# A down-projection by seven block products: four of eight feature pairs instead of three

## The reference, cut to what matters

```python
f = jnp.square(jax.nn.relu(u @ w_up[l])) @ w_down[l]     # (256, 8192) @ (8192, 2048)
h = h + rms_norm(f, g_post_mlp[l])
```

## Time and profile before

| | |
|---|---|
| median of 3 runs | 2031.14 us (2030.65 to 2031.42) |
| the profiled execution | 2031.48 us, of which the span is 2029.7 us |
| PE busy | 2017.8 us, 99% of the span, 10509 matmuls |
| DVE busy | 1489.5 us, 73% |
| ACT busy | 985.2 us, 49% |
| mean granted clock of TensorE | 0.999 |
| HBM read | 385.02 MB, 191 GB/s over the span |

### The profile page before, as it was taken

The page is one execution under the profiler, slowest core; times in us unless marked ns, Lnnn a source line. Parts: engine busy times, 40 slices in busy tenths (PEclk is TensorE's granted clock), DMA queues, the critical chain, the costliest instruction groups (busy, mean ns, idle before and its releaser), DMA issues.

```text
span 2029.7 us, 28875 instructions
## 1 busy us (share of the span) xinstructions
PE 2017.8 (99%) x10509; PEld 1719.2 (85%) x10509; DVE 1489.5 (73%) x2016; ACT 985.2 (49%) x1275; POOL 83.0 (4%) x91
## 2 busy tenths in 40 slices
PE   9999999999999999999999999999999999999998
PEld 7888898888888888999888888888888888888886
DVE  6766766566756655578999856587877887788887
ACT  6645444565544544433444644554553453354343
POOL 0000102001002000002000000000000000000001
PEclk9999999999999999999999999999999999999999
DMA  9688655655667665555666566655576466467554
GB/s 346 198 202 185 177 157 174 187 175 173 185 198 245 185 196 179 175 177 160 189 198 199 177 219 185 192 166 174 185 236 188 158 206 217 155 207 227 187 198 134
DMA packets 265475, 389.32 MB, mean 192 GB/s; under 512 B 12504, under 2 KB 147032, under 8 KB 264571
## 3 DMA queue, kind: packets, MB, share of 16 engines
q1 hardware_dynamic: 262587, 377.19, 60.9%
q0 software_dynamic: 2624, 10.54, 1.9%
q10 hardware_dynamic: 144, 0.01, 0.0%
HBM read 385.02 MB, written 2.54 MB: 191 GB/s over the span
## 4 chain that ended last, share of the span: by engine, by line
PE 98%; SPq 1%; DMA 1%; DVE 0%; ACT 0%; issue 0%; DVEq 0%
PE acc L701 18%; PE acc L678 17%; PE acc L680 17%; PE acc L679 17%; PE acc L699 10%; PE acc L692 2%; PE acc L691 2%; PE acc L693 2%; PE acc L697 1%; PE aux L730 1%; PE aux L732 1%; PE aux L731 1%; PE acc L730 1%; PE acc L731 1%; PE acc L732 1%; PE aux L1619 1%
## 5 line engine op out<-in xcount | busy, mean ns | idle before, releaser
L532 DVE TENSOR_TENSOR low_rows<-stage_rows,high_rows 128x1024 fp32r<-128x1024 f32 x480 | 575.2, 1210 | 295.6 <-ACT high_rows L518 286.9
L518 ACT ACTIVATE high_rows<-stage_rows 128x1024 fp32r<-128x1024 f32 x480 | 495.5, 1040 | 542.2 <-PE acc L680 480.8
L518 ACT ACTIVATE w_high<-stage 128x1024 fp32r<-128x1024 f32 (+1 forms) x264 | 276.1, 1047 | 405.1 <-PE acc L701 298.0
L532 DVE TENSOR_TENSOR w_low<-stage,w_high 128x1024 fp32r<-128x1024 f32 (+1 forms) x264 | 319.8, 1221 | 176.1 <-ACT w_high L518 171.5
L701 PE MATMUL acc<-u,w_high 128*128 128x512 f32 x900 | 247.9, 394 | 0.0
L701 PE MATMUL acc<-hT,w_high 128*128 128x512 f32 x645 | 177.5, 394 | 0.0
L701 PEld LDWEIGHTS acc<-u,w_high 128*128 128x128 f32 x900 | 152.9, 189 | 19.0
L699 PEld LDWEIGHTS acc<-u,w_low 128*128 128x128 f32 x960 | 146.8, 188 | 20.5
L699 PE MATMUL acc<-u,w_low 128*128 128x256 f32 x960 | 152.5, 281 | 0.0
L678 PE MATMUL acc<-high_rows,hT 128*128 128x512 f32 x384 | 151.8, 395 | 0.0
L680 PE MATMUL acc<-high_rows,hT 128*128 128x512 f32 x384 | 149.6, 390 | 0.0
(11 more groups left out here) (451 smaller groups left out, 3601.4 us busy)
## 6 DMA issues: line engine op xcount, KB each, us to landing
stage_rows<-in_w_in SPq DMA_DIRECT2D x160, 512.0 KB, 3.8
stage<-in_w_in SPq DMA_DIRECT2D x136, 512.0 KB, 3.6
stage_rows<-in_w_down SPq DMA_DIRECT2D x128, 512.0 KB, 4.4
stage<-in_w_up SPq DMA_DIRECT2D x120, 512.0 KB, 4.5
stage_rows<-in_w_o SPq DMA_DIRECT2D x64, 512.0 KB, 4.1
stage_rows<-in_w_pool_out SPq DMA_DIRECT2D x16, 512.0 KB, 3.9
stage_rows<-in_w_conv_out SPq DMA_DIRECT2D x16, 512.0 KB, 4.4
stage_rows<-in_w_mem_kv SPq DMA_DIRECT2D x14, 512.0 KB, 11.2
```

The lines of the kernel that those rows point to most:

```text
L518: act.activation(high[:, pr, k_from:kt, 0:p.cols], src[:, slot, k_from:kt, 0:p.cols], ACT.Copy).then_inc(high_done, 1)
L532: dve.tensor_tensor(low[:, pr, k_from:kt, 0:p.cols], src[:, slot, k_from:kt, 0:p.cols], high[:, pr, k_from:kt, 0:p.cols].bitcast(F32), ALU ...
```

## The change

Pairs 2, 3, 5 and 6 are done by seven products instead of 2, 4 and 6. A step of w_down has 24 slabs then, where it had 22, and the order of its pairs is: plain 0 and 1, seven 2, seven 3, plain 4, seven 5, seven 6, plain 7.

The kept rows are not added up by VectorE any more. Ahead of a step, ScalarE writes the rows kept in `z_rows` into the banks `aux` (`lay_z`: four copies, in the second step of a quarter at slabs 0 and 1, for the first step in the stage w_up before, at slabs 4 and 5); TensorE goes on summing in the banks (no start flag, from step 2 on; it waits for `z_laid` at the first LEFT); and after each step ScalarE copies the banks out (`keep_z`, in all quarters). Of the place of `f_sums` in memory one part is moved, since it is larger by a third.

```diff
--- before.py
+++ after.py
@@ -128,7 +128,7 @@
 
 
 LEFT, RIGHT, OUTER, INNER = "left", "right", "outer", "inner"
-SEVENS = (2, 4, 6)
+SEVENS = (2, 3, 5, 6)
 SEVEN_ORDER = ((0, 1), (2,), (3,), (4,), (5,), (6,), (7,))
 
 
@@ -278,7 +278,8 @@
         u2 = at("u2", Z + 48, [P, KT, 2, T], F32R)
         f_pair = at("f_pair", Z + 84, [P, KT, 2, T], F32R)
         y_rows = at("y_rows", Z + 16, [P, 2, D])
-        f_sums = at("f_sums", Z + 32, [P, len(SEVENS), 2, 4, P], F32R)
+        sums_at = [(Z + 32 + 4 * e, Z + 34 + 4 * e) for e in range(3)] + [(74.25, 82.75)]
+        f_sums = [[at(f"f_sums{e}{half}", kb, [P, 4, P], F32R) for half, kb in enumerate(places)] for e, places in enumerate(sums_at)]
         f_raw = at("f_raw", 72.25, [P, 4, P])
         z_at = ((Z + 44, Z + 46, Z + 80, Z + 82), (Z + 116, Z + 118, Z + 120, 80.75))
         z_rows = [[at(f"z_rows{step}{b}", kb, [P, ROW]) for b, kb in enumerate(places)] for step, places in enumerate(z_at)]
@@ -712,24 +713,24 @@
             (_, one, _), (_, two, _) = (job.group(i, u, part) for part in range(2))
             if kind == LEFT:
                 pe.wait_ge(s("f_sums_ready"), len(SEVENS) * int(job.name[-1]) + e + 1)
-                if e == 0 and step:
-                    if step <= 2:
-                        pe.wait_ge(s("z_copied"), 4 * step)
-                    else:
-                        pe.wait_ge(s("z_summed"), 4 * (step - 2))
+                if e == 0 and step == 1:
+                    pe.wait_ge(s("z_copied"), 4)
+                elif e == 0 and step:
+                    pe.wait_ge(s("z_laid"), 4 * (step - 1))
             pe.wait_ge(split_done, STAGES + n + 1)
             x1, x2 = ([p.rows[:, k0, half, 0:P] for half in range(2)], [p.rows[:, k0 + 1, half, 0:P] for half in range(2)])
             x4 = [p.rows[:, k0 + 1, half, P:2 * P] for half in range(2)]
-            sums = [[f_sums[:, e, half, r, :] for half in range(2)] for r in range(4)]
+            sums = [[f_sums[e][half][:, r, :] for half in range(2)] for r in range(4)]
             products = {LEFT: [(0, x1, aux[:, 0, :], True), (1, x2, acc[:, 2 * one, :], False)],
                         RIGHT: [(1, sums[3], acc[:, 2 * two, :], False)],
                         OUTER: [(turned, sums[1], aux[:, 1, :], True), (1 - turned, sums[0], aux[:, 3, :], True)],
                         INNER: [(0, sums[2], aux[:, 2, :], True), (1, x4, acc[:, 2 * one + 1, :], False)]}[kind]
             for k, (x_high, x_low), bk, own in products:
                 high, low = high_rows[:, pr, k, :], low_rows[:, pr, k, :]
-                pe.matmul(bk, x_high, high, start=own and e == 0, stop=False)
-                pe.matmul(bk, x_high, low, start=False, stop=False)
-                mm = pe.matmul(bk, x_low, high, start=False, stop=own and e == len(SEVENS) - 1)
+                laid = own and step >= 2
+                pe.matmul(bk, x_high, high, start=own and e == 0 and not laid, stop=False, skip_group_check=laid)
+                pe.matmul(bk, x_high, low, start=False, stop=False, skip_group_check=laid)
+                mm = pe.matmul(bk, x_low, high, start=False, stop=own and e == len(SEVENS) - 1, skip_group_check=laid)
             mm.then_inc(used, 1)
 
         def group_done(eng, job, i, u, part=0):
@@ -1437,7 +1438,7 @@
             def beside_last(n):
                 r = SQUARE_ROWS_AT.get(n)
                 if r is not None:
-                    act.wait_ge(s("z_summed"), 21)
+                    act.wait_ge(s("z_spread"), 1)
                     down_squares(r)
 
             def down_squares(r):
@@ -1452,20 +1453,35 @@
                         act.wait_ge(s("chain_var"), 11 + t)
                         act.activation(out_rs[:, t:t + 1], out_rs[:, t:t + 1], ACT.Sqrt).then_inc(s("chain_root"), 1)
 
-            def copy_z(q):
+            def lay_z(q, step, banks):
+
+                act.wait_ge(s("z_copied"), 4 * (2 * q + step))
+                for b in banks:
+                    act.activation(aux[:, b, :], z_rows[step][b][:], ACT.Copy).then_inc(s("z_laid"), 1)
+
+            def keep_z(q):
                 job = jobs[f"w_down{q}"]
                 inner = max(idx for idx, kind in enumerate(job.kinds) if kind == INNER)
 
                 def beside(n):
                     step, idx = n // job.S, n % job.S
-                    for b in {inner: (0, 1), inner + 2: (2, 3)}.get(idx, ()):
+                    if q and step and idx < 2:
+                        lay_z(q, step, (2 * idx, 2 * idx + 1))
+                    for b in {inner: (0, 1), inner + 1: (2, 3)}.get(idx, ()):
                         act.wait_ge(used, PAIRS + job.slab0 + step * job.S + inner + 1)
                         act.activation(z_rows[step][b][:], aux[:, b, :], ACT.Copy).then_inc(s("z_copied"), 1)
                 return beside
 
+            def lay_first(q):
+
+                def beside(n):
+                    if n in (4, 5):
+                        lay_z(q, 0, (2 * n - 8, 2 * n - 7))
+                return beside
+
             for q in range(4):
-                rounding(f"w_up{q}", beside=beside_up0 if q == 0 else None)
-                rounding(f"w_down{q}", beside=copy_z(q) if q == 0 else None)
+                rounding(f"w_up{q}", beside=lay_first(q) if q else beside_up0)
+                rounding(f"w_down{q}", beside=keep_z(q))
             rounding("w_down_last", last_down, beside=beside_last)
 
 
@@ -2576,8 +2592,8 @@
                 link(dve.tensor_tensor(f_raw[:, 0:2, :], f[:, 0:4:3, :], f[:, 1:2, :].to_broadcast([P, 2, P]), ALU.subtract))
                 link(dve.tensor_tensor(f_raw[:, 2, :], f_raw[:, 1, :], f[:, 0, :], ALU.add))
                 link(dve.tensor_tensor(f_raw[:, 3, :], f[:, 2, :], f_raw[:, 2, :], ALU.subtract))
-                link(dve.tensor_copy(f_sums[:, e, 0], f_raw[:]))
-                dve.tensor_tensor(f_sums[:, e, 1], f_raw[:], f_sums[:, e, 0].bitcast(F32), ALU.subtract).then_inc(s("f_sums_ready"), 1)
+                link(dve.tensor_copy(f_sums[e][0][:], f_raw[:]))
+                dve.tensor_tensor(f_sums[e][1][:], f_raw[:], f_sums[e][0][:].bitcast(F32), ALU.subtract).then_inc(s("f_sums_ready"), 1)
 
             def down_body(q, name, first=0):
                 job = jobs[name]
@@ -2615,32 +2631,15 @@
                     link(dve.tensor_tensor(y21, y21, z7[:], ALU.add))
                     link(dve.tensor_tensor(y22, y22, z5[:], ALU.subtract))
 
-            def sum_z(q):
-                job = jobs[f"w_down{q}"]
-                inner = max(idx for idx, kind in enumerate(job.kinds) if kind == INNER)
-
-                def beside(n):
-                    step, idx = n // job.S, n % job.S
-                    for b in {inner + 1: (0, 1), inner + 2: (2, 3)}.get(idx, ()):
-                        if b == 0:
-                            dve.wait_ge(used, PAIRS + job.slab0 + step * job.S + inner + 1)
-                            if q == 1:
-                                dve.wait_ge(s("z_copied"), 4 * (step + 1))
-                            else:
-                                dve.wait_ge(s("z_summed"), 8 * (q - 2) + 4 * (step + 1))
-                        v = z_rows[step][b]
-                        dve.tensor_tensor(v[:], aux[:, b, :], v[:], ALU.add).then_inc(s("z_summed"), 1)
-                return beside
-
             def spread(name, step, n):
                 if n in SPREAD_AT[name]:
-                    dve.wait_ge(s("z_summed"), 16 if step else 20)
+                    dve.wait_ge(s("z_copied"), 24 if step else 28)
                     z_spread(step, SPREAD_AT[name].index(n))
 
             def beside_last(n):
                 spread("w_down_last", 0, n)
                 if n == SPREAD_AT["w_down_last"][-1]:
-                    dve.sem_inc(s("z_summed"), 1)
+                    dve.sem_inc(s("z_spread"), 1)
 
             def last_down():
 
@@ -2673,7 +2672,7 @@
             splitting("w_up_first", first_body, beside=beside_first, at_once=True)
             for q in range(4):
                 splitting(f"w_up{q}", up_body(f"w_up{q}", 0 if q else 2), 3, beside=sums_up(q), at_once=True)
-                splitting(f"w_down{q}", down_body(q, f"w_down{q}"), beside=sum_z(q) if q else None, at_once=True)
+                splitting(f"w_down{q}", down_body(q, f"w_down{q}"), at_once=True)
                 if q == 0:
                     dve.wait_ge(s("h2_squared"), 8)
                     link(dve.tensor_reduce(eps_3, sums_3, AX, ALU.add))
```

## The result

The changed kernel takes 2049.79 us (median of 6 runs, 2048.55 to 2051.19), the one before 2030.89 us beside it (2030.51 to 2031.71). The ratio is 1.0093, with a 95% interval of 1.008 to 1.0106: slower by 18.9 us. The forecast was 2048.2 us.

The account below looks back on a forecast made before the run. TensorE, busy 88.00 of 88 us in the down-projections, was taken to bound the kernel. New waits of 21.8 us less 4.76 us saved gave +17.1 on 2031.14: 2048.2 us, range 2042 to 2056.

Parts of the forecast that it names:

- The gain: 21 matmuls by 0.2267, 4.76 us: TensorE in w_down: one more pair takes 7 products instead of 8 in each of 7 steps, saving 4.76 us.
- The wait at OUTER of every second seven, 1.41 us, and its restart, 0.15 us: TensorE at a couple's second OUTER: ready at 8.21, wanted at 6.80; 1.56 us with restart, 14 times, 21.8 us.
- The start at 2.71: VectorE starts the second seven's LEFT 2.71 us after the first's first matmul, set by a buffer; a 5.50 us chain follows.
- rival A: The cover holds at the second seven's OUTER, so only the gain is left: 2026.4 us; chance 0.08.
- The pitch of 1.14 us against a full duration of 1.22: Queued VectorE operations start 1.14 us apart; counting 1.22 would add 0.16 us per couple, 2 us in all.
- INNER just in time: 0: Second seven's INNER: low part ready at 9.44, TensorE wants it at 9.50; counted 0, up to 0.3 us in the range.
- C: Larger waits: INNER's margin fails (4.2 us) and ScalarE's copies cost 5 us: 2057.4 us; chance 0.07.
- Writes and copies by ScalarE: 0: ScalarE's 20 writes into banks and 28 copies out, near 0.585 us each, are hidden: 0; 5 us if cover failed.
- The feature sums in w_up: 0: One more pair's feature sums cost VectorE 2.3 us per w_up stage; counted 0, at worst 1.0 us once in w_up3.
- DMA: 0: Loads and bytes per step stay; the tightest load in a step lands at 12.6, wanted near 18: 0.
- B: Smaller waits: half of each wait at OUTER is absorbed, +6.2 us, 2037.3 us; chance 0.07.
- D: TensorE's clock falls to 1.2 GHz for 12 matmuls after each of 14 waits, +38 us: 2086 us; chance 0.03.

Follow-up runs that it names:

- e7_sums_ahead_two_couples: Changed kernel with the addition for OUTER and the first for INNER moved earlier on VectorE, pair order kept: 2027.76 us, ratio 0.9983 to the kernel before.
- e3_outer_ahead: Changed kernel with only the addition for OUTER moved on VectorE, ahead of the low part of the slab before LEFT: 2033.61 us, ratio 1.0012 to the kernel before.
- e2_scalar_alone: Changed kernel with sevens 2, 4, 6 only, keeping ScalarE's writes and copies of kept rows: 2030.91 us, ratio 1.0 to the kernel before.
- e1_one_couple: Changed kernel with sevens 2, 3, 5, so three sevens and one back-to-back couple a step: 2042.35 us, ratio 1.0056 to the kernel before.
- e6_order: Changed kernel with four sevens (2, 3, 4, 6) reordered so only 3 and 4 stand back to back: 2039.34 us, ratio 1.0042 to the kernel before.
- e5_order_and_sums_ahead: Changed kernel with sevens 2, 3, 4, 6, only 3 and 4 adjacent, and OUTER's and the first INNER addition moved earlier: 2027.62 us, ratio 0.9985 to the kernel before.
- e8_loads_not_held: Changed kernel with SyncE issuing each next w_up load once its own buffer is free: 2050.81 us, ratio 1.0094 to the kernel before.
- e4_sums_on_gpsimd: Changed kernel with all additions of weight blocks for OUTER and INNER given to GpSimd: 2066.63 us, ratio 1.0175 to the kernel before.

## Why the prediction was right, point by point

**The gain: 21 matmuls by 0.2267, 4.76 us.** Right in count (10488 against 10509). The two runs without waits in w_down show -3.4 and -3.3 us in the time, not -4.8, and the rows say where the rest is. From the first LEFT to the start of the last matmul TensorE takes 591.89 us in the kernel before and 588.27 in e7_sums_ahead_two_couples, 3.62 us less. The other 1.14 us lie nearly all at the second seven of each couple: 10.25 us from its LEFT to the next instead of 10.20 in the couple 2, 3, and some 0.1 us too long in the couple 5, 6, where the second matmul of OUTER starts up to 0.30 us after the first. Its low part is ready only some 0.1 us ahead; why that costs a restart isn't shown. So the price of 0.2267 us a matmul holds, and what fits so narrowly isn't quite free.

**The wait at OUTER of every second seven, 1.41 us, and its restart, 0.15 us.** Right in place, number and size. The wait seen is 1615.74 less 1614.27, 1.47 us, with another 0.11 at the second matmul and some 0.02 in the matmuls after: 1.60 against 1.56. The rows say 14 x 1.60 = 22.4 us, I had 21.8. The first experiment shows the position to be the cause, the third shows that the chain is: what is taken out of it comes off the wait at full length.

The start at 2.71 was the step that the whole forecast hung on (the buffer, not VectorE's time). It is at 2.72. Had it been a question of VectorE's time, moving the sum would have returned nothing. That the buffer sets this start is read from the rows: ScalarE begins 1.62 after t = 0 in both kernels, each time released by the products' last line. No run gave it a fifth buffer, which would test it directly. "Idle time before it can't be used", which the prediction held against rival A, is true of the order in this code only: e3_outer_ahead used that very time.

**The pitch of 1.14 us against a full duration of 1.22.** The rows after have 1611.33 and 1612.47 for the outer sum, again 1.14, and the wait came out as summed by it. The Trainium skill, "VectorE: DVE Perf Modes", section "The DRAIN you can't avoid", says first that an operation doesn't start before the pipe of the former is empty. Taken as the full duration at the two places that the prediction names, that gives an estimate of 8.37 for the end of the chain; it is at 8.23. (The 14 couples would make 2.2 us of it, where the prediction says 2.) The same section goes on that an operation which isn't held starts earlier, which the prediction left out; the rows agree, and by how much had to be read from them.

**INNER just in time: 0.** Right: no wait before INNER in any of the 14. But the sum had a slip. With OUTER begun at 8.28 its six matmuls of 1.36 us end at 9.64, not 9.50. In the rows INNER's low part is ready at 9.43, as forecast (9.44), and INNER begins at 9.76: the margin is 0.33 us instead of 0.06, so that C's first half was less near than it seemed.

**Writes and copies by ScalarE: 0.** Right, shown by e2_scalar_alone. The write into a bank, which no trace of before had, took 0.583 us, and I had taken 0.585.

**The feature sums in w_up: 0.** No wait stands there.

**DMA: 0.** This term was wrong, by 0.9 us. I looked for the tightest load within a step. The one that mattered is at the step's end: SyncE's program holds the first loads of the next w_up until the inner sums of the last seven are through. In the trace after, at the edge of w_down2 and w_up3, the last inner sum is on VectorE at 1852.19, for 0.69 us, and SyncE's row of loads begins 0.41 behind its end; the loads land some 4 us later, and ScalarE waits for them. SyncE, VectorE's sum, ScalarE:

```profile
1853.29 7.37 SPq L506 DMA_DIRECT2D stage<-in_w_up  x8
```

```profile
1852.19 0.69 DVE L551 TENSOR_TENSOR stage_rows<-stage_rows 128x512 f32<-128x512 f32 x1
```

```profile
1857.19 1.06 ACT L519 ACTIVATE w_high<-stage 128x1024 fp32r<-128x1024 f32 x1 [1.32 <-DMA stage<-in_w_up]
1858.99 1.06 ACT L519 ACTIVATE w_high<-stage 128x1024 fp32r<-128x1024 f32 x1 [0.73 <-DMA stage<-in_w_up]
```

And what came of it, on VectorE (the additions to y_rows) and on TensorE:

```profile
1861.23 1.28 DVE L2612 TENSOR_TENSOR y_rows<-acc,y_rows 128x512 f32<-128x512 f32 x2
```

```profile
1862.14 0.39 PE L681 MATMUL acc<-high_rows,f_pair 128*128 128x512 f32 x1
1862.70 0.49 PE L698 MATMUL acc<-u,w_high 128*128 128x512 f32 x1 [0.17 <-DVEq L2614]
```

ScalarE had to wait 1.32 and 0.73 us for weights of w_up, where the kernel before has no wait for a DMA at this edge (at that of w_down0 and w_up1 it has two, of 0.30 and 0.69 us, and no gap of TensorE). So VectorE's low parts, which stand ahead of the additions to y_rows on its queue, were late, the additions ended at 1862.5, and TensorE's first product of w_up, which needs their bank, started at 1862.70 instead of 1862.37, with 0.1 us of restart. At the three edges that makes 0.35, 0.1 and 0.43 us. In e1_one_couple, e6_order and e5_order_and_sums_ahead, whose steps do not end in a couple, there is no such gap, and in e8_loads_not_held, which takes the hold away and leaves all else, it is gone at all three edges. What stays open is why the time of that run did not show it.

The account: 14 x 1.60 + 0.9 - 4.76 = 18.5 us; the start of the kernel was 0.4 us quicker in this execution; 18.1 us is the difference of the spans. The median's 18.9 us lies within the spread of the runs about that.

**The rivals.** A (the cover holds) did not occur here, and its point of decision was the right one: the chain had to fit into the 4.09 us between 2.71 and 6.80. In e7_sums_ahead_two_couples 3.56 us of it are left behind LEFT, with 3.69 to be had from its start at 3.11, and it fits. B and C were sizes, and the forecast's own was met. D, the clock, stayed at 0.999 in spite of 14 waits of 1.3 us.

## What to carry to other kernels

Where engines hand slabs through a ring of buffers, an average (VectorE busy in 76 of 88 us) says nothing of a burst: take the item whose buffer frees last, add the chain behind it in the order of the queue, and compare with the time until it is wanted. A cheaper product that needs more preparation costs time where two of them stand back to back, and the cure is to find the piece of preparation that needs no buffer and to put it into the idle time ahead. Two additions moved ahead did it here: 22.0 us, with no work saved.

## What the runs showed of the hardware

GpSimd's additions slow VectorE's subtractions when both work on this memory. With the additions running beside it in e4_sums_on_gpsimd, VectorE's subtraction of 1024 columns took 1.746 us on average instead of 1.222, and work worth 73 us on VectorE cost 94 us there when it was given away. The Trainium skill, "GPSIMD Engine Reference", section "Specifications", names the shared access and contention with VectorE instructions of two SBUF inputs, as these are; this trace agrees, and the factor of 1.4 to 2.1 on the average is its own.

The average hides how it comes about. Two subtractions that follow each other on VectorE, and GpSimd's addition, which begins between their starts:

```profile
1622.17 1.22 DVE L531 TENSOR_TENSOR low_rows<-stage_rows,high_rows 128x1024 fp32r<-128x1024 f32 x1
1623.31 3.43 DVE L531 TENSOR_TENSOR low_rows<-stage_rows,high_rows 128x1024 fp32r<-128x1024 f32 x1
```

```profile
1622.82 2.84 POOL L544 TENSOR_TENSOR stage_rows<-stage_rows 128x1024 f32<-128x1024 f32 x1 [8.51 <-DMA stage_rows<-in_w_down]
```

The addition ends at 1625.66 and the second subtraction at 1626.74, 1.08 later. So it is with every subtraction in w_down that took longer than in the changed kernel: 50 of 1024 columns end 1.08 or 1.09 us after the end of an addition, 18 of 512 columns 0.55 us after it, whenever they began; the others took 1.26 us at most, and 0.68. They look as if they had stood still until the addition was over, and had then run at full speed.

TensorE's clock held through waits of 1.3 us in the changed kernel, and in e4_sums_on_gpsimd through waits of up to 2.13 us (granted clock 1.00 until 1975.7). After one of 2.29 us it fell in the same run (TensorE's timeline; the two fast matmuls behind the wait and two slow ones):

```profile
1971.84 0.39 PE L681 MATMUL acc<-high_rows,f_pair 128*128 128x512 f32 x1
1974.52 0.47 PE L679 MATMUL acc<-high_rows,f_pair 128*128 128x512 f32 x1 [2.29 <-DVE low_rows L531]
1974.82 0.39 PE L680 MATMUL acc<-low_rows,f_pair 128*128 128x512 f32 x1
...
1976.19 0.63 PE L679 MATMUL acc<-high_rows,f_pair 128*128 128x512 f32 x1
1976.62 0.63 PE L680 MATMUL acc<-low_rows,f_pair 128*128 128x512 f32 x1
```

From 1975.8 to 1979.2, where the granted clock is 0.51, the matmuls start 0.43 us apart, the pace at 1.2 GHz, nearly twice the 0.2267 at 2.4 GHz; some eight matmuls of 0.2 us more, 1.6 us on top of the wait. It is the only fall in this profile between the first matmuls and the last stretch; the mean granted clock of the run's four executions is 0.996 to 0.998. This is the case that rival D was about, in a run in which TensorE stood longer than in the changed kernel; the Trainium skill, "TensorE: Matmul & The Clock Gate", section "HAM oscillation — how this bites in real kernels", tells of a kernel whose clock fell behind waits for DMA, waits that were longer than this one. This trace agrees that it can fall behind a wait, and here it did so behind 2.29 us, once, and not behind 2.13.
